# Seven block products instead of eight in the branch projections of a one-core decoder trunk

## The chip, the core and the metric

The kernel runs on one core of one Trainium2 chip. TensorE (PE) multiplies, VectorE (DVE) and ScalarE (ACT) prepare operands and take results out of PSUM, SyncE (SP) issues most DMAs and ACT the rest; GpSimd (POOL) is not used. Each engine works through its own list in order and waits on semaphores. The metric is the device time of one execution, in microseconds (us).

## The reference

512 tokens, 2048 channels, all in float32. Cut to what matters here:

```
h = rmsnorm(x); proj = h @ w_in                  # 2048 -> 18 blocks x 8 heads x 128, and 3 x 2048 gates
gates = sigmoid(proj[gate part] + gate_b)        # 3 x [512, 2048]
ya = diff_attention(...)  * silu(az)             # [512, 1024] each
yb = dilated_attention(...) * silu(bz)
yc = cb * conv3(cc * cx) * silu(cz)
merged = gates[0] * (ya @ w_branch_a) + gates[1] * (yb @ w_branch_b) + gates[2] * (yc @ w_branch_c)
out = rmsnorm(x + merged @ w_out, final_g)
```

## The kernel before

A float32 product is done as three matmuls on parts: high parts by high parts, high by low, low by high (`three`, L419 to L421). So every weight unit (128 x 1024 words, 512 KB) goes through the same line: SP loads it into one of three `raw` slots, ACT makes its high part `w_hi` (L698, L702), DVE the low part `w_lo` = raw - w_hi (L1007, L1011), PE uses both. All three tiles are rings of three, so unit r can be split only after PE is done with unit r-3, and its load can start only after the low part of unit r-3 is made.

Four stages follow each other:

- **Heads.** 8 heads, each of 18 steps (a projection block of two units, 24 matmuls each) with the attention work put between the steps. Head 0 and head 7 are written out, heads 1 to 6 are a loop. `turn` has PE transpose into two alternating PSUM tiles `tr_ps`; before turn number idx it waits until the turns up to idx-2 have been read out (`t_free`). In each head DVE forms the four weight sums for the output projection (`sum_out_units`, L1044 to L1047, at step 7): ACT loads 2 MB of `wo` into `ssum` at step 2 and stores the sums to `s_dram` at step 8.
- **Gates.** 2048 x 6144, done with 7 block products instead of 8 (a Winograd form of Strassen's scheme): 6 quads of 28 units, 12 matmuls each. The sums of the activation blocks (f1, f2, f4, f3, of 128 x 2048) are formed by DVE around the change of stage (`combine_h`, L1345, L1346) and split like weights (`comb_high`, `comb_low` L1039). The four sums of weight blocks of each quad are formed by DVE beside them (`add_units`). `take_g` (L1323) evicts a product into up to four tiles of `gin`; ACT applies tanh and stores the gates to `g_dram`.
- **Branches.** `y @ w_branch` for three branches, in 12 groups (branch, column group of 512) of 4 units, with 24 matmuls a unit: 8 k-tiles x 4 token tiles x 3. Four banks belong to a group, the other four to the next. The branch activations come from `y_dram` (`load_y`, L337, 2 MB in rows of 2 KB) and are split once per branch. `take_group` reads the four banks: (gate+1) times the bank (L1366), and for branches 1 and 2 an addition to `merged` (L1373).
- **Output.** `merged @ w_out`, transposed by PE and copied by ACT (`copy_merged`, L904), again 7 block products: 2 quads of 28 units. `take_o` (L1404) evicts; the blocks of `merged` and their sums are split at the start of this stage. A final norm follows.

The order of the work is written out by hand in each engine's program; no planner is used.

Of the kernel before, what the change touches and what calls it, by code (L numbers as in the profile page):

```python
# [58 lines left out]
GROUPS, NU = 12, 4  # L59
R_G = W1  # L60
R_B = R_G + QUADS_G * STEPS
R_O = R_B + GROUPS * NU
X_B = 8 * QUADS_G
X_O = X_B + GROUPS * NU
W11, W12, W21, W22 = range(4)
ON_X, ON_Z, ON_Y = range(3)
# [7 lines left out]
S_ORDER = [2, 3, 0, 1]  # L74
# [11 lines left out]
def spot(s):  # L86
    return S_ORDER.index(s)

# [14 lines left out]
def program(nc, wst, wg, wb, wo, x_t, x_tok, cols_d, rows_d, lam_d, const_d, out_d):  # L103
# [4 lines left out]
    s_dram = nc.dram_tensor("s_dram", (HEADS, 4, P, HU), f32, kind="Internal").ap()  # L108

    with ExitStack() as ctx:  # L110
# [74 lines left out]
        with ExitStack() as c2:  # L185
            s2 = sb_in(c2)
            s2("below2", [P, KT * T])
# [14 lines left out]
        def part(tile, n):  # L202
# [12 lines left out]
        y_parts = [[tile[:, 4096 * n:4096 * (n + 1)].rearrange("p (k q) -> p k q", k=8) for n in at]  # L215
                   for tile, at in ((tb, (0, 1)), (kb_r, (1, 2)))] + [[act_hi[:, 0:8, :], act_hi[:, 8:16, :]]]
        y_raw = kb[:, 0:4096].rearrange("p (k q) -> p k q", k=8)
        merged = act_lo_f[:, :, :].rearrange("p (s k) q -> p s (k q)", s=4)

        m_t = tb_f[:, 0:8192].rearrange("p (k q) -> p k q", k=KT)  # L220
        flat_hi = act_hi[:, :, :].rearrange("p k q -> p (k q)")
        flat_gin = gin[:, :, :].rearrange("p k q -> p (k q)")
        o11 = [part(tb, 4), part(tb, 5)]
        o_t1, o_t2, o_t4 = [[part(kb_r, n), part(kb_r, n + 1)] for n in (0, 2, 4)]
        o_t3 = [part(gin_r, n) for n in (0, 1)]
        o21, o22 = [[part(flat_hi, n), part(flat_hi, n + 1)] for n in (0, 2)]
        operands_o = [o11, o_t1, o_t2, o21, o_t3, o22, o_t4]
        g1f, g4f, g3f = part(kb, 3), part(kb, 5), part(flat_gin, 1)
        m11, m12 = [m_t[:, 0:8, h * H:(h + 1) * H] for h in range(2)]
        m21, m22 = [m_t[:, 8:16, h * H:(h + 1) * H] for h in range(2)]  # L230
        res = merged

# [5 lines left out]
        sets = [sc_ps + tr_ps, [o_ps] + pb]  # L238
# [8 lines left out]
        yraw_in, gin_in = sem("yraw_in"), [sem(f"gin_in{i}") for i in range(2)]  # L247
# [20 lines left out]
        yhi_done, ylo_done = sem("yhi_done"), sem("ylo_done")  # L268
# [20 lines left out]
        def _(sp):  # L289
# [49 lines left out]
            def load_gates(g):  # L339
                b, cg = divmod(g, 4)  # L340
                sp.dma_start(gin[:, 4 * (g % 2):4 * (g % 2) + 4, :],
                             g_dram[b, :, :, C * cg:C * (cg + 1)].rearrange("s p q -> p s q")).then_inc(gin_in[g % 2], 16)
# [28 lines left out]
            sp.wait_ge(ylo_done, 4)  # L371
            load_y(1)
            for g in range(GROUPS):
                for u in range(NU):
                    ring_free(X_B + NU * g + u)
                    load_ring(X_B + NU * g + u, wb[g, u, :, :])
                    if g < 2 and u == 3:
                        for n in range(4 * g, 4 * g + 4):
                            sp.wait_ge(g_stored[n], 16 * QUADS_G)
                        load_gates(g)  # L380
                    if g >= 2 and u == 2:
                        if g < 6:
                            sp.wait_ge(m_got, 4 * (g - 1))
                        else:
                            sp.wait_ge(m_added, 4 * (g - 5))
                        load_gates(g)
                    if g == 2 and u == 0:
                        sp.wait_ge(ylo_done, 8)
                        load_y(2)
                    if g == 3 and u == 0:  # L390
                        sp.dma_start(rows[:, :], rows_d[0:1, 3 * D:4 * D].to_broadcast([P, D])).then_inc(grow_in, 16)
            for q in range(QUADS_O):
                for n in range(STEPS):
                    p, u = divmod(n, NU)
                    x = X_O + STEPS * q + n
                    ring_free(x)
                    load_ring(x, wo[NU * q + u, (W11, None, None, W12, None, None, W22)[p], :, :] if p in (0, 3, 6) else
                              s_dram[NU * q + u, (None, W22, W11, None, W21, W12, None)[p], :, :])
# [15 lines left out]
        def _(pe):  # L414
# [173 lines left out]
            def product(r, operand, banks, p, free=None, between=None):  # L588

                hi, lo = operand  # L590
                for u in range(NU):
                    pe.wait_ge(lo_done, r + NU * p + u + 1)
                    slot = (r + NU * p + u) % RING
                    for s in range(2):
                        if free and u == 0:
                            pe.wait_ge(free[0], free[1][s])
                        for kk in range(2):
                            k, ts, cs = 2 * u + kk, slice(P * s, P * (s + 1)), slice(C * kk, C * (kk + 1))
                            end = three(banks[s][:, :], hi[:, k, ts], lo[:, k, ts], w_hi[slot][:, cs], w_lo[slot][:, cs],
                                        FRESH[p] and k == 0, k == 7, True)  # L600
                    end.then_inc(pe_used, 1)
                    if between:
                        between(u)
# [11 lines left out]
            for q in range(QUADS_G):  # L615
                for p in range(PRODUCTS):
                    if q == 0 and p in (1, 2, 4):
                        pe.wait_ge(comb_lo, {1: 1, 2: 2, 4: 4}[p])
                    product(R_G + STEPS * q, operands_g[p], pairs[(q + CHAIN[p]) % 3], p, free_g(q, p))

            def turn_merged(g, s):

                cg = g % 4
                pe.wait_ge(m_added, 4 * (g - 4) + spot(s) + 1)
                for kk in range(4):
                    end = nc.tensor.transpose(sets[g % 2][s][:, P * kk:P * (kk + 1)],
                                              merged[:, s, C * cg + P * kk:C * cg + P * (kk + 1)], ident[:, :])
                end.then_inc(m_turned, 1)

            for g in range(GROUPS):  # L630
                if g % 4 == 0:
                    pe.wait_ge(ylo_done, g + 4)
                y_hi, y_lo = y_parts[g // 4]
                for u in range(NU):
                    r = R_B + NU * g + u
                    pe.wait_ge(lo_done, r + 1)
                    slot = r % RING
                    for s in range(4):
                        if u == 0:
                            if g == 0:  # L640
                                pe.wait_ge(got, evicted(QUADS_G - 1, (5, 3)[s // 2], s % 2))
                            elif g == 1:
                                pe.wait_ge(got, evicted(QUADS_G - 1, 6, 1))
                            else:
                                pe.wait_ge(m_got, 4 * (g - 2) + spot(s) + 1)
                            if g >= 10:
                                pe.wait_ge(m_copied, 4 * (g - 10) + spot(s) + 1)
                        for kk in range(2):
                            k, ts, cs = 2 * u + kk, slice(P * s, P * (s + 1)), slice(C * kk, C * (kk + 1))
# [37 lines left out]
        def _(act):  # L687
# [219 lines left out]
            for g in range(GROUPS):  # L907
                for u in range(NU):
# [9 lines left out]
                    if g == 0:  # L918
                        high_y(1, u)
# [637 lines left out]
```

## Time and profile before

| | us |
|---|---|
| median of 3 runs (lowest, highest) | 2647.27 (2647.14, 2648.31) |
| profiled execution, own time | 2650.81 |
| its span | 2649.0 |
| PE busy | 2617.0 |
| DVE busy | 1554.4 |
| ACT busy | 866.9 |

The granted clock of PE was 0.995 of full speed over the span. A row of the timeline gives start, duration, engine, line and operation; the duration of a matmul is longer than its share of the pipe, so the pace is read from the starts. Times in all rows count from the start of the span, which begins a little after the execution's own time does.

### The profile page before, as it was taken

What the parts mean: (1) busy time and instruction counts of PE and PEld (TensorE: products, weight loads), DVE (VectorE), ACT (ScalarE), POOL (GpSimd) and SP (SyncE); (2) the same over time, 40 slices, a digit from 0 to 9 for tenths busy, and PEclk for the clock granted to TensorE, in tenths of its full rate; (3) what the DMA queues carried; (4) which work ended last, traced back from release to release, by engine and by line L of the source; (5) the groups of instructions that cost most, each with busy time, mean ns of one, the idle gap of its engine ahead of it and who ended that gap; (6) DMA issues with size and microseconds to landing.
All of it is one profiled execution on the core that took longest, in us unless ns stands there. A gap on an engine that the chain in (4) does not pass through costs nothing.

```text
span 2649.0 us, 31176 instructions
## 1 busy us (share of the span) xinstructions
PE 2617.0 (99%) x11986; PEld 2161.9 (82%) x11986; DVE 1554.4 (59%) x1910; ACT 866.9 (33%) x1089; POOL 0.2 (0%) x4
## 2 busy tenths in 40 slices
PE   8999999999999999999999999999999999999998
PEld 6888888888888888888888888878888888888786
DVE  6563654554455356365455446788877784444775
ACT  5322232322222232223232222334444443212454
POOL 0000000000000000000000000000000000000000
PEclk9999999999999999999999999999999999999999
DMA  5323333332342432333234234335455446444565
GB/s 211 119 87 100 119 123 96 119 130 85 124 131 81 135 119 87 100 120 123 96 119 130 85 124 131 135 111 191 167 185 181 161 134 246 159 144 142 186 192 195
DMA packets 102819, 359.31 MB, mean 136 GB/s; under 512 B 10017, under 2 KB 10274, under 8 KB 100770
## 3 DMA queue, kind: packets, MB, share of 16 engines
q1 hardware_dynamic: 82352, 296.49, 34.2%
q10 hardware_dynamic: 20338, 60.89, 6.3%
q8 instruction: 107, 1.75, 0.3%
q14 instruction: 22, 0.18, 0.0%
HBM read 317.50 MB, written 39.85 MB: 135 GB/s over the span
## 4 chain that ended last, share of the span: by engine, by line
PE 96%; DVE 3%; SPq 0%; DMA 0%; ACT 0%; issue 0%; DVEq 0%; ACTq 0%
PE proj L419 22%; PE proj L421 22%; PE proj L420 22%; PE sc_ps L419 3%; PE sc_ps L421 3%; PE sc_ps L420 3%; PE tr_ps L419 3%; PE tr_ps L421 3%; PE tr_ps L420 3%; PE o_ps L420 2%; PE o_ps L421 2%; PE o_ps L419 2%; PE tr_ps L460 2%; PE sc_ps L452 1%; PE o_ps L505 1%; PE sc_ps L491 1%
## 5 line engine op out<-in xcount | busy, mean ns | idle before, releaser
L419 PE MATMUL proj<-act_hi,w_hi 128*128 128x512 f32 x2304 | 910.9, 395 | 8.1 <-DVE act_lo L1055 8.1
L421 PE MATMUL proj<-act_hi,w_lo 128*128 128x512 f32 x2304 | 900.4, 391 | 0.0
L420 PE MATMUL proj<-act_lo,w_hi 128*128 128x512 f32 x2304 | 899.8, 391 | 0.0
L1007 DVE TENSOR_TENSOR w_lo<-raw,w_hi 128x1024 fp32r<-128x1024 f32 x288 | 352.7, 1225 | 400.6 <-ACT w_hi L698 400.1
L698 ACT ACTIVATE w_hi<-raw 128x1024 fp32r<-128x1024 f32 x288 | 304.6, 1058 | 842.6 <-PE proj L421 837.9
L419 PEld LDWEIGHTS proj<-act_hi,w_hi 128*128 128x128 f32 x2304 | 434.3, 189 | 96.4 <-issue 9.0
L421 PEld LDWEIGHTS proj<-act_hi,w_lo 128*128 128x128 f32 x2304 | 434.1, 188 | 92.1
L420 PEld LDWEIGHTS proj<-act_lo,w_hi 128*128 128x128 f32 x2304 | 434.7, 189 | 86.9
L1011 DVE TENSOR_TENSOR w_lo<-raw,w_hi 128x1024 fp32r<-128x1024 f32 x152 | 185.7, 1223 | 220.6 <-ACT w_hi L702 220.6
L702 ACT ACTIVATE w_hi<-raw 128x1024 fp32r<-128x1024 f32 x152 | 161.2, 1061 | 354.9 <-PE proj L421 148.2
L702 ACT ACTIVATE w_hi<-kb 128x1024 fp32r<-128x1024 f32 x120 | 127.2, 1061 | 185.2 <-PE proj L421 64.4
L1011 DVE TENSOR_TENSOR w_lo<-kb,w_hi 128x1024 fp32r<-128x1024 f32 x120 | 146.5, 1222 | 57.7 <-ACT w_hi L702 57.7
L765 ACT ACTIVATE sc<-sc,nmax 128x768 f32<-128x768 f32 (+4 forms) x96 | 65.5, 683 | 182.0 <-DVE nmax L1152 101.9
L1138 DVE TENSOR_TENSOR stage<-proj,rstd 128x512 f32<-128x512 f32 x40 | 27.6, 691 | 97.8 <-PE proj L421 97.8
L419 PE MATMUL tr_ps<-w_hi,act_hi 128*128 128x512 f32 x192 | 74.7, 389 | 0.0
L420 PE MATMUL tr_ps<-w_lo,act_hi 128*128 128x512 f32 x192 | 74.7, 389 | 0.0
L779 ACT ACTIVATE qk_hi<-stage 128x512 fp32r<-128x512 f32 x32 | 20.2, 632 | 151.7 <-DVE stage L1138 107.8
L419 PE MATMUL sc_ps<-w_hi,act_hi 128*128 128x512 f32 x160 | 63.1, 394 | 2.5 <-DVE w_lo L1011 2.5
L1136 DVE TENSOR_TENSOR stage<-proj,rstd 128x512 f32<-128x512 f32 x24 | 26.3, 1095 | 64.6 <-PE proj L421 64.6
L420 PE MATMUL sc_ps<-w_lo,act_hi 128*128 128x512 f32 x160 | 62.7, 392 | 0.0
L419 PE MATMUL sc_ps<-w_hi,tb 128*128 128x512 f32 x144 | 56.4, 392 | 1.6 <-issue 1.5
L419 PE MATMUL proj<-w_hi,act_hi 128*128 128x512 f32 x144 | 56.2, 391 | 0.9 <-DVE w_lo L1011 0.9
(294 smaller groups left out, 3343.3 us busy)
## 6 DMA issues: line engine op xcount, KB each, us to landing
raw<-wst SPq DMA_DIRECT2D x288, 512.0 KB, 3.5
raw<-wg SPq DMA_DIRECT2D x48, 512.0 KB, 4.0
raw<-wb SPq DMA_DIRECT2D x48, 512.0 KB, 3.6
kb<-wg SPq DMA_DIRECT2D x10, 2048.0 KB, 7.7
ssum<-wo ACTq DMA_DIRECT2D x8, 2048.0 KB, 9.5
s_dram<-ssum ACTq DMA_DIRECT2D x8, 2048.0 KB, 7.5
raw<-s_dram SPq DMA_DIRECT2D x32, 512.0 KB, 3.3
kb<-wg SPq DMA_DIRECT2D x24, 512.0 KB, 6.2
```

The source lines that it names most:

```text
L419: nc.tensor.matmul(out, w_h, a_h, start=first, stop=False, skip_group_check=shared)
L420: nc.tensor.matmul(out, w_h, a_l, start=False, stop=False, skip_group_check=shared)
L421: return nc.tensor.matmul(out, w_l, a_h, start=False, stop=last, skip_group_check=shared)
L452: end = nc.tensor.matmul(sc_ps[m][:, 0:n], q_part[AQ][rows, qs], k_part[AK][rows, 0:n], start=step == 0, stop=step == 2)
L460: end = nc.tensor.transpose(tr_ps[idx % 2][:, n * P:(n + 1) * P], tile, ident[:, :])
L491: end = nc.tensor.matmul(sc_ps[1][:, (g - 1) * P:g * P], blk[q][:, qs], blk[k][:, qs], start=True, stop=True)
L698: nc.scalar.activation(w_hi[slot_w][:, :], raw[slot_raw][:, :], ACT.Copy).then_inc(hi_done, 1)
L702: nc.scalar.activation(w_hi[r % RING][:, :], src, ACT.Copy).then_inc(hi_done, 1)
L765: end = nc.scalar.activation(tile[:, lo:hi], tile[:, lo:hi], ACT.Exp, scale=scale, bias=nmax[:, m:m + 1], accum_out=sums[:, m:m + 1])
L1007: tt(w_lo[slot_w][:, :], raw[slot_raw][:, :], w_hi[slot_w][:, :].bitcast(f32), ALU.subtract).then_inc(lo_done, 1)
L1011: tt(w_lo[r % RING][:, :], src, w_hi[r % RING][:, :].bitcast(f32), ALU.subtract).then_inc(lo_done, 1)
L1138: ins = tt(blk[w][:, :], pb[w % RING][:, :], rstd[:, :], ALU.mult)
```

## The change

The branch projections also get 7 block products. A branch is two quads: 4 k-tiles x 256 tokens by 4 k-tiles x 512 columns per block, so a product has 2 units of 12 matmuls and a quad 14 units. The order within a quad is P1, P2, P6, P5, P7, P3, P4. P1 and P6, P7, P4 share one chain of banks, P5 and P3 another, P2 has a third; ACT copies the first results out (`first_of`), DVE adds or subtracts the later ones (`finish`) in a tile `rows` in SBUF and then gates them.

The weight sums of the branches are formed like those of the output, in the heads: 12 + 8 sets of four sums, three sets per head (steps 7, 12 and 16; two in head 0, none in head 7). The activation sums of a branch (`sum_y`) are formed by DVE. Two of the gates' activation sums move: f4 is begun at unit 3 of the first gates quad and ended at unit 17, f3 is formed at units 8 to 11 by three operations instead of two; half of the first weight sums move from step 17 to step 16 of the last head.

```diff
-GROUPS, NU = 12, 4
+QUADS_B, STEPS_B, NU = 6, 14, 4
+ORDER_B = [P1, P2, P6, P5, P7, P3, P4]
+GATED = [0, 3, 1, 2]
+SUM_AT = {7: 0, 12: 1, 16: 2}
...
@@ SP, the loads
-            sp.wait_ge(ylo_done, 4)
-            load_y(1)
-            for g in range(GROUPS):
-                for u in range(NU):
-                    load_ring(X_B + NU * g + u, wb[g, u, :, :])
...
+            for qb in range(QUADS_B):
+                for n in range(STEPS_B):
+                    load_unit(X_B + STEPS_B * qb + n, 2 * qb + n % 2, ORDER_B[n // 2])
...
+                    if (qb, n) == (0, 9):
+                        sp.wait_ge(ylo_done, 6)
+                        load_y(1)
+                    if (qb, n) == (2, 6):
+                        sp.wait_ge(ylo_done, 7 + 6)
                         load_y(2)
...
@@ ACT, the heads
-                    if w == 2:
-                        act.dma_start(ssum[:, :, :], wo[...]).then_inc(osum_in, 16)
-                    if w == 8:
-                        act.dma_start(s_dram[...], ssum[:, :, :]).then_inc(osum_stored, 16)
+                    if w in (4, 9, 14) and not last and not (fresh and w == 14):
+                        act.dma_start(ssum[:, :, :], ws[...]).then_inc(osum_in, 16)
+                    if w - 1 in SUM_AT and not last and not (fresh and w == 17):
+                        act.dma_start(s_dram[...], ssum[:, :, :]).then_inc(osum_stored, 16)
...
@@ DVE, the heads
-                    if w == 7:
-                        sum_out_units(i)
+                    if w in SUM_AT and not last and not (fresh and w == 16):
+                        sum_units(SUM_AT[w] if fresh else 3 * i + (SUM_AT[w] - 1))
...
@@ ACT, the branches
+            def first_of(qb, p):
+                act.wait_ge(pe_used, RING + R_B + STEPS_B * qb + 2 * ORDER_B.index(p) + 2)
...
+                for s in range(2):
+                    nc.scalar.activation(parts[2 * SLOT[d] + s], bank[s][:, :], ACT.Copy, scale=float(sign)).then_inc(d_first, 1)
...
@@ DVE, the branches
+            def finish(qb, p):
+                d, first, op = {P2: (0, P1, ALU.add), P7: (3, P5, ALU.subtract), P3: (1, P6, ALU.add)}[p]
...
+                for s in range(2):
+                    tt(parts[2 * SLOT[d] + s], parts[2 * SLOT[d] + s], bank[s][:, :], op).then_inc(d_added, 1)
+                gate(qb, d)
...
+                    elif n == 0:
+                        finish(qb - 1, P3)
+                    elif n == 3:
+                        finish_last(qb - 1)
+                    if n == 6:
+                        finish(qb, P2)
+                    if n == 12:
+                        finish(qb, P7)
```

How it moves the work on DVE at two places. First, step 12 of head 0, where `w_lo` is the low part of a unit, `v_lo` reads a transposed block out of `tr_ps` and `stage` evicts the step's projection. Before:

```order
L1180 TENSOR_SCALAR pr<-sc,rsum 128x768
L1007 TENSOR_TENSOR w_lo<-raw,w_hi 128x1024
L1185 TENSOR_TENSOR v_lo<-tr_ps,v_hi 128x512
L1136 TENSOR_TENSOR stage<-proj,rstd 128x512
L1007 TENSOR_TENSOR w_lo<-raw,w_hi 128x1024
```

And now:

```order
L1253 TENSOR_SCALAR pr<-sc,rsum 128x768
L1085 TENSOR_TENSOR w_lo<-raw,w_hi 128x1024
L1122 TENSOR_TENSOR ssum<-ssum 128x1024
L1123 TENSOR_TENSOR ssum<-ssum 128x1024
L1124 TENSOR_TENSOR ssum<-ssum 128x1024
L1125 TENSOR_TENSOR ssum<-ssum 128x1024
L1258 TENSOR_TENSOR v_lo<-tr_ps,v_hi 128x512
L1209 TENSOR_TENSOR stage<-proj,rstd 128x512
L1085 TENSOR_TENSOR w_lo<-raw,w_hi 128x1024
```

The four sums now stand ahead of the read of `tr_ps` and ahead of the eviction; heads 1 to 6 have the same order. Second, the branch stage of DVE. Before, between two low parts of a group there is at most one `take_group`; here the end of a group in branch 1:

```order
L1011 TENSOR_TENSOR w_lo<-raw,w_hi 128x1024 x4
L1366 SCALAR_TENSOR_TENSOR gin<-gin,tr_ps 128x512 x2
L1366 SCALAR_TENSOR_TENSOR gin<-gin,sc_ps 128x512 x2
L1373 TENSOR_TENSOR act_lo_f<-act_lo_f,gin 128x512 x4
L1011 TENSOR_TENSOR w_lo<-raw,w_hi 128x1024 x4
```

Now, from unit 12 of quad 3 to unit 3 of quad 4 (branch 1 into branch 2; `rows` holds the partial results, `kb_r` the low part of a block of y):

```order
L1089 TENSOR_TENSOR w_lo<-raw,w_hi 128x1024
L1480 TENSOR_TENSOR rows<-rows,sc_ps 128x512 x2
L1464 SCALAR_TENSOR_TENSOR gin<-gin,rows 128x512 x2
L1471 TENSOR_TENSOR act_lo_f<-act_lo_f,gin 128x512 x2
L1089 TENSOR_TENSOR w_lo<-raw,w_hi 128x1024
L1417 TENSOR_TENSOR kb_r<-kb,kb_r 128x1024
L1089 TENSOR_TENSOR w_lo<-raw,w_hi 128x1024
L1480 TENSOR_TENSOR rows<-rows,tr_ps 128x512 x2
L1464 SCALAR_TENSOR_TENSOR gin<-gin,rows 128x512 x2
L1471 TENSOR_TENSOR act_lo_f<-act_lo_f,gin 128x512 x2
L1089 TENSOR_TENSOR w_lo<-raw,w_hi 128x1024
L1417 TENSOR_TENSOR kb_r<-kb,kb_r 128x1024
```

Six operations follow the low parts of units 12 and 0 there, each with a low part of y behind them, and a unit now has 12 matmuls and not 24.

## Rows read from the trace of the kernel before

**Rows 1.** The page: busy time and instructions; the chain that ended last, by engine.
```profile
PE 2617.0 (99%) x11986; PEld 2161.9 (82%) x11986; DVE 1554.4 (59%) x1910; ACT 866.9 (33%) x1089; POOL 0.2 (0%) x4
...
PE 96%; DVE 3%; SPq 0%; DMA 0%; ACT 0%; issue 0%; DVEq 0%; ACTq 0%
```

**Rows 2.** Windows, from the gates to the last matmul: us, busy (x), PEclk, DMA share, GB/s.
```profile
1743.31:1796.37 53.06, 47.91 (x193) 37.61 (x192) 51.95 (x44) 21.10 (x19) 0.00 (x0) 0.94 0.25 85
1796.37:2209.81 413.44, 413.44 (x1825) 342.15 (x1823) 324.80 (x310) 186.64 (x199) 0.00 (x0) 1.00 0.50 171
2209.81:2211.50 1.69, 0.16 (x1) 0.03 (x1) 1.23 (x1) 1.69 (x4) 0.00 (x0) 1.00 0.37 148
2211.50:2478.02 266.52, 266.52 (x1200) 221.46 (x1201) 119.47 (x134) 70.79 (x74) 0.00 (x0) 1.00 0.48 162
2478.02:2638.13 160.11, 156.81 (x689) 128.42 (x687) 115.16 (x114) 78.98 (x93) 0.00 (x0) 0.99 0.60 198
```

**Rows 3.** Timeline of PE, two products of a gates quad: start us, us, operation.
```profile
1807.25 0.39 PE L419 MATMUL tr_ps<-w_hi,act_hi 128*128 128x512 f32 x1
...
1818.13 0.39 PE L419 MATMUL sc_ps<-w_hi,tb 128*128 128x512 f32 x1
```

**Rows 4.** Timeline of DVE in one head: the sums, and steps 12 and 13.
```profile
971.13 1.22 DVE L1044 TENSOR_TENSOR ssum<-ssum 128x1024 f32<-128x1024 f32 x1
...
975.92 1.07 DVE L1136 TENSOR_TENSOR qk<-proj,rstd 128x512 f32<-128x512 f32 x1
...
1029.76 1.22 DVE L1007 TENSOR_TENSOR w_lo<-raw,w_hi 128x1024 fp32r<-128x1024 f32 x1 [1.78 <-ACT w_hi L698]
...
1030.90 0.68 DVE L1185 TENSOR_TENSOR v_lo<-tr_ps,v_hi 128x512 fp32r<-128x512 f32 x1
...
1034.59 1.12 DVE L1136 TENSOR_TENSOR stage<-proj,rstd 128x512 f32<-128x512 f32 x1 [3.01 <-PE proj L421]
```

**Rows 5.** Timeline of PE at the end of that step 12.
```profile
1035.52 0.82 PE L460 MATMUL tr_ps<-ident,pr 128*128 128x128 f32 x6
1036.09 0.48 PE L419 MATMUL proj<-act_hi,w_hi 128*128 128x512 f32 x1
```

**Rows 6.** Timeline of PE after the heads; in brackets the wait before.
```profile
1754.09 0.79 PE L419 MATMUL sc_ps<-w_hi,act_hi 128*128 128x512 f32 x1 [2.46 <-DVE w_lo L1011]
...
1755.54 0.63 PE L419 MATMUL sc_ps<-w_hi,act_hi 128*128 128x512 f32 x1
...
1755.97 0.63 PE L420 MATMUL sc_ps<-w_lo,act_hi 128*128 128x512 f32 x1
```

**Rows 7.** Timeline of DVE there.
```profile
1755.09 2.28 DVE L1345 SCALAR_TENSOR_TENSOR act_lo_f<-tb_f,act_hi 128x2048 f32<-128x2048 f32 x1
...
1759.62 1.22 DVE L1011 TENSOR_TENSOR w_lo<-kb,w_hi 128x1024 fp32r<-128x1024 f32 x1
```

**Rows 8.** DMA issues of SP before the branch stage: start us, us, operation.
```profile
2196.47 0.44 SPq L337 DMA_DIRECT2D kb<-y_dram  x1
2198.82 12.94 SPq L310 DMA_DIRECT2D raw<-wb  x4
```

**Rows 9.** Timeline of ACT there.
```profile
2209.08 1.06 ACT L702 ACTIVATE w_hi<-raw 128x1024 fp32r<-128x1024 f32 x1 [6.11 <-DMA raw<-wb]
```

**Rows 10.** DMA from 2195 to 2215 us: GB/s in 40 slices of 0.5 us.
```profile
GB/s 0 0 0 0 106 82 238 270 258 336 299 361 291 356 393 414 406 406 401 406 406 406 422 401 414 401 401 410 426 410 229 90 0 348 373 201 143 287 434 303
```

**Rows 11.** Timeline of DVE in the branch stage, one evicted group.
```profile
2322.90 1.28 DVE L1366 SCALAR_TENSOR_TENSOR gin<-gin,tr_ps 128x512 f32<-128x512 f32 x2
...
2325.29 2.49 DVE L1373 TENSOR_TENSOR act_lo_f<-act_lo_f,gin 128x512 f32<-128x512 f32 x4
```

**Rows 12.** Timeline of ACT in the output stage: one copy pair.
```profile
2487.42 1.06 ACT L904 ACTIVATE tb_f<-proj 128x512 f32<-128x512 f32 x2
```

**Rows 13.** Timeline of PE in the output stage: the longest wait.
```profile
2504.13 0.47 PE L419 MATMUL sc_ps<-w_hi,kb_r 128*128 128x512 f32 x1 [2.40 <-DVE act_lo_f L1404]
```

**Rows 14.** Waits of the run: us in total, times, longest us.
```profile
PE proj L419 <- DVE w_lo L1011: 0.9, 2, 0.6
```

More of the change, by code:

```diff
@@ L231, in program @@
         res = merged
+        parts = [rows[:, C * n:C * (n + 1)] for n in range(4)]
         pb = [ctx.enter_context(nc.psum_tensor(f"proj{i}", [P, T], f32)) for i in range(RING)]
@@ L585, in _, with product @@
                 blocks(i, 0)
-            def product(r, operand, banks, p, free=None, between=None):
+            def product(r, operand, banks, p, free=None, after=None, nu=NU):
                 hi, lo = operand
-                for u in range(NU):
-                    pe.wait_ge(lo_done, r + NU * p + u + 1)
-                    slot = (r + NU * p + u) % RING
+                for u in range(nu):
+                    pe.wait_ge(lo_done, r + u + 1)
+                    slot = (r + u) % RING
                     for s in range(2):
@@ L616, in _ @@
                 for p in range(PRODUCTS):
[L617 to L649, printed above, removed]
-                            end = three(sets[g % 2][s][:, :], y_hi[:, k, ts], y_lo[:, k, ts], w_hi[slot][:, cs],
-                                        w_lo[slot][:, cs], k == 0, k == 7)
-                    end.then_inc(pe_used, 1)
-                    if g >= 9 and u == 1:
-                        for s in S_ORDER:
-                            turn_merged(g - 1, s)
@@ new lines, in _, with turn_merged @@
+                    product(R_G + STEPS * q + NU * p, operands_g[p], pairs[(q + CHAIN[p]) % 3], p, free_g(q, p))
+            def turn_merged(qb, d):
+                pair = qb % 2
+                for s in range(2):
+                    n = gated(qb - 4, d, s)
+                    pe.wait_ge(m_added, gated(qb - 2, d, s))
+                    if n > 2:
+                        pe.wait_ge(m_copied, n - 2)
+                    c0 = C * (2 * pair + d // 2)
+                    for kk in range(4):
+                        end = nc.tensor.transpose(pairs[3][s][:, P * kk:P * (kk + 1)],
+                                                  merged[:, 2 * (d % 2) + s, c0 + P * kk:c0 + P * (kk + 1)], ident[:, :])
+                    end.then_inc(m_turned, 1)
@@ new lines, in turns_b, with after @@
+            def turns_b(qb, n):
+                def after(u):
+                    at = n + u
+                    if qb >= 4 and at == 8:
+                        turn_merged(qb, 0)
+                    if qb == 5 and at in (0, 2, 5):
+                        turn_merged(4, {0: 3, 2: 1, 5: 2}[at])
+                return after
+            for qb in range(QUADS_B):
+                for i, p in enumerate(ORDER_B):
+                    if qb % 2 == 0:
+                        pe.wait_ge(ylo_done, 7 * (qb // 2) + i + 1)
+                    product(R_B + STEPS_B * qb + 2 * i, operands_y[qb // 2][p], pairs[(QUADS_G + qb + CHAIN[p]) % 3], p,
+                            free_b(qb, p), turns_b(qb, 2 * i), 2)
@@ L1295, in _ @@
             head(0)
-            links = steps["n"] - before - 1
+            links = steps["n"] - before - 1 + 2
             with dve.Fori(1, HEADS - 1) as i:
```

462 lines of the change are left out of this document (277 added, 185 removed).

## The prediction

> **What bounds the kernel now.** I read the page's shares first: PE is busy 2617.0 of 2649.0 us, and the chain that ended last is PE for 96% and DVE for 3% [rows 1]. So time goes only where matmuls go or where PE waits. Then the windows by stage and, inside them, the timeline of PE for its pace and waits. The pace: two products of a gates quad, 48 matmuls, lie 10.88 us apart, 0.2267 us each [rows 3]. With it each stage can be held against its matmul count. Branch stage: 1152 matmuls x 0.2267 = 261.2, the window is 266.52 [rows 2]; the rest, 5.3 us, is 48 transposes at 0.11, so PE never waits there, DVE being busy 119 us of it. Gates, first part: 16 units should take 16 x 2.72 = 43.5 and take 53.06, a loss of 9.5. Between gates and branches 1.69 passes with one matmul in it. Output: 672 x 0.2267 = 152.3, plus 16 transposes 1.8, stands at 160.11: a loss of 6.0 [rows 2, 3]. The rest of the gates window (413.44) has 1824 matmuls x 0.2267 = 413.5 and no wait. All losses of PE after the heads are 17 us, at the changes of stage, and there DVE or a DMA is late.
>
> **The matmuls.** A branch is now 2 quads x 7 products x 2 units x 12 = 336 matmuls instead of 384; over three branches 1008 instead of 1152. 144 x 0.2267 = 32.6 us less. They are of the same shape, in a stage without waits, so all of it is on the path. Transposes stay 64. This is the one large term.
>
> **The heads.** The sums per head go from one set to three: 12 more sets in all, 4 operations each. A set takes 975.92 - 971.13 = 4.79 us on DVE [rows 4], 57 us in sum, and 48 MB more go over the ACT queue. At step 7 one set already hides. At step 16 DVE stands idle about as long as at step 12, the set delays an eviction by some 1.6, and nothing is read from `tr_ps` after it: nothing. At step 12 the set stands ahead of `v_lo`. In the trace `v_lo` starts at 1030.90, with the set at 1035.69, and ends 0.68 later at 1036.37. The eviction then starts 1.8 late (1036.3 for 1034.59); DVE had idled 3.01 before it [rows 4], and the idle time of step 13 takes up what is left. But PE's second turn after step 12 may only start when `v_lo` has read its bank. Six transposes run from 1035.52 to 1036.09, 0.095 each, so the second turn (the last two) starts at 1035.90 [rows 5]: PE waits 0.47. Seven heads have this set: +3.3. Ends: 0 (DVE's read may release earlier than its row ends; PE did not wait here before, so there is nothing to gain) and 7 x 1.8 = 12.6 if the late eviction reached PE as well. I take 3.3.
>
> **Heads to gates.** DVE is behind here: unit 3's low part comes 2.46 late, and f3's two operations (1755.09 to 1759.62, 2.27 each) stand ahead of the low part of unit 4 [rows 6, 7]. After the 2.46 wait the starts are 0.43 apart, 1.2 GHz, for eight matmuls: 1.6 us. The change takes half of f4 and two weight sums (4.6 us) out of step 17, and puts six block operations instead of five between units 3 and 13. I went through the units with 1.14 for a low part (1029.76 to 1030.90 [rows 4]), 1.13 for a weight sum, 2.2 to 2.3 for a block operation: unit 3 is late by 0.1, 4 by 1.9 (f4 before it), 5 by 1.8 (low part of the second block), then 0.4, 0.3, 0.7, 0.4, 0.4, at 14 1.8 (low part of f3) and at 15 0.9: 8.5 for 9.5 before. -1.0; ends -4 and +2 (the clock falls at these waits too).
>
> **Gates to branches.** Before the branches SP issues `load_y(1)` at 2196.47, then the first weights at 2198.82; ACT gets them at 2209.08, after 6.11 of waiting [rows 8, 9], and PE loses 1.69 - 0.2 = 1.5 [rows 2]. The load moves away from here, and the y blocks needed first were loaded one stage earlier: -1.5. It moves to unit 9 of quad 0, where its surroundings are the same: again a 2.72 us pace, again the next weight load issued 2.4 us behind 2 MB in the same queue, landing 10.1 us after its issue where 5.9 are free and 9.0 just do without PE waiting. So I put 1.5 there. `load_y(2)` was hidden before by the 5.44 us pace of a 24-matmul unit; at unit 6 of quad 2 the pace is 2.72 and it costs 1.5 as well. +3.0; ends 0 (the slices after 2203 us ran at 400 GB/s [rows 10]) and 8 (gate loads in the same queue).
>
> **Inside the branch stage.** A low part may come 3.2 us late before PE waits (5.44 for two units, less 1.06 for ACT, 1.14 for DVE); each 2.72 us step leaves DVE 1.58 for other work. A pair of 128x512 operations takes 1.2 (1.28 for two, 2.49 for four [rows 11]), so an eviction is 2.4 in branch 0 and 3.6 later, a low part of a y block 1.14. Quads 0 to 2 never pile up over 2.5. Quad 3 is worst: it makes branch 2's y blocks beside evictions of 3.6. Unit 12 starts 0.2 behind and leaves 2.2, unit 13 1.8, unit 0 of quad 4 adds 3.6 and leaves 3.8, so unit 1 is at least 0.6 late; with some 0.1 for each dependent step I take 1.2. Ends 0 and 6 (each of four such seams). At the end of quad 5 stand the sum of the first output block, two low parts (2.2 each) and evictions of 3.6: 0.6, 1.2, 3.3, 3.9 behind; the output's first product waits 1.3 for its bank, its second unit 0.6: +1.9, ends 0 and 4. Before, the same low parts lay in 5.44 us steps.
>
> **Output.** The longest wait, 2.40 [rows 13], is for the eviction of P1, behind three low parts of blocks. The change puts one more copy pair of ACT (1.06 [rows 12]) ahead of the first of them: +0.9, ends 0 and 3. The two waits of 0.9 together [rows 14] stay.
>
> **The sum.** -32.6 + 3.3 - 1.0 - 1.5 + 3.0 + 1.2 + 1.9 + 0.9 = -24.8. Profiled execution: 2650.81 - 24.8 = 2626.0. The median of the runs shown is 3.54 below that execution: 2647.27 - 24.8 = 2622.5.
>
> **Rivals.** *Waits hide better* (B): the turn in the heads is released in time, and the y loads are absorbed by the slack of the ring. 2622.5 - 3.3 - 3.0 = 2616. For it: 400 GB/s in the late slices [rows 10] against some 250 wanted. Against: the same order of loads did make PE wait once.
>
> *Short waits lower the clock* (C). PE will have about 7 waits of 0.5 in the heads and 10 of 1 to 3 later. Only waits of 2.4 us and more were followed by starts 0.43 apart; after the 1.5 us before the branches the pace stayed 0.23, and the window from there shows a clock of 1.00 [rows 2, 6]. If the five waits of 1.5 to 1.9 (the y loads, units 4, 5 and 14 of the gates) cost 1.6 each: +8, 2630.5. If every wait did: (7 + 8) x 1.6 = +24, 2646.5, no change at all (C').
>
> The Trainium skill speaks for C: "TensorE: Matmul & The Clock Gate", section "A second HAM failure mode: psum-queue depth-cycling", tells of a kernel whose PE idled for moments between matmul groups while cycling through banks and whose clock swung between its two levels. The products here now cycle three bank pairs every 24 matmuls; by that rule the sum would go to C'. The gates stage cycles the same way at a clock of 1.00 [rows 2], so the trace speaks against it as long as the waits are short.
>
> *The weight stream starves the branches* (D, slower). The stage now wants 84 x 0.524 + 24 x 0.524 (gates) + 2 x 2.1 (y) = 60.8 MB in 228.5 + 4.4 + 4.2 = 237 us, 256 GB/s; before, 162, and the output stage, the only one like it, ran at a mean of 198 [rows 2]. At 198 the stage would take 307 us: 2692. It decides against the change from 60.8 / (237 + 24.8) = 232 GB/s down. Against: slices of 400 and more over 7 us [rows 10], and the output stage lost almost nothing to its loads.
>
> The Trainium skill would add to D: "DMA: Bandwidth & Descriptors", section "Bandwidth", asks for transfers of 1 MiB and more for three quarters of the peak, and the gates now come in 24 loads of 512 KB instead of 12 of 1 MB. The sum is not changed by it: the 400 GB/s were reached with 512 KB loads in the mix.
>
> *The change does not do what it says*: the program has the 1008 matmuls; ruled out.
>
> **Chances.** Forecast 0.58 (its own range 2618 to 2628), B 0.17, C 0.13, C' 0.05, D 0.05, 0.02 for something better still. A change within 0.2%, about what a measurement of this kernel cannot tell from none, is 2642.0 to 2652.6: C' alone. Faster 0.90, same 0.05, slower 0.05. The range takes in B and C: 2614 to 2634.
>
> **What would show it.** The window from the first branch matmul to the first of the output at 237 to 240 us; a wait of about 0.5 before the transposes at step 12 of heads 0 to 6 on DVE's `v_lo`, none in head 7; a wait for a low part whose high part waited for `raw`, near units 10 of quad 0 and 7 of quad 2; one near unit 1 of quad 4 with DVE busy throughout; nothing before the first branch product. The forecast is wrong if PE waits at every seam of a quad, if the clock of the branch window is under 0.97, or if a head is longer by more than 1 us.

## The result, and the profile after

The changed kernel takes 2665.23 us (median of 4 runs, 2660.11 to 2669.44), the kernel before 2647.79 in the same comparison. The ratio is 1.0064, 95% interval 1.0053 to 1.0076: slower by 17 us, where 2622.5 had been forecast. The profiled execution of the changed kernel is its fastest, 2660.11 with a span of 2658.3; against the span before that is +9.3. Of the four runs two lie near 2661 and two near 2669; those two show a mean granted clock of 0.989 to 0.990, the profiled one 0.994, so what slows this kernel also varies from run to run.

The page of the changed kernel, the lines that answer to [rows 1]:

```profile
PE 2592.6 (98%) x11842; PEld 2134.2 (80%) x11842; DVE 1698.7 (64%) x2052; ACT 935.9 (35%) x1182; POOL 0.2 (0%) x4
...
PE 89%; DVE 5%; DMA 2%; issue 2%; ACT 1%; SPq 0%; DVEq 0%; ACTq 0%
```

PE is busy 24.4 us less, though the 144 matmuls that are gone were worth 32.6: in the branch stage it is busy 31.8 less, up to the end of the heads 7.2 more (1739.26 for 1732.03, with the same 8082 matmuls), where part of the matmuls ran at the slower clock. And the span is longer: PE now idles 66 us instead of 32, and the chain has DVE, DMA and "issue" in it. The question is where. The windows of the stages, answering to [rows 2] (first 16 units of the gates, the rest of the gates, branches, output; the passage between gates and branches is gone):

```profile
1773.88:1826.22 52.34, 46.54 (x194) 35.26 (x193) 50.88 (x43) 19.18 (x18) 0.00 (x0) 1.00 0.23 78
1826.22:2239.66 413.44, 413.44 (x1826) 342.34 (x1825) 336.53 (x320) 191.62 (x204) 0.00 (x0) 1.00 0.50 171
2239.66:2481.21 241.55, 234.74 (x1049) 192.53 (x1048) 199.73 (x221) 137.23 (x162) 0.00 (x0) 1.00 0.75 252
2481.21:2647.46 166.25, 158.46 (x696) 129.25 (x696) 116.80 (x116) 80.29 (x97) 0.00 (x0) 0.99 0.61 204
```

The branch stage is 241.55 us for 266.52, 25.0 less. The start of the gates gains 0.7, the passage to the branches 1.7, the output stage loses 6.1 (166.25 for 160.11). That is -21.3 in all, and it does not explain a slower kernel. The gates begin at 1773.88 instead of 1743.31: 30.6 us are lost in the heads, where the prediction had put 3.3.

One head of the changed kernel, from one values product to the next, cut where PE stands still:

```profile
868.23:891.68 23.45, 23.45 (x111) 19.32 (x109) 13.69 (x15) 3.19 (x3) 0.00 (x0) 1.00 0.43 152
891.68:895.09 3.41, 0.00 (x0) 0.01 (x1) 2.85 (x4) 1.58 (x2) 0.00 (x0) 1.00 0.88 268
895.09:899.66 4.57, 4.57 (x13) 3.62 (x14) 0.61 (x3) 0.00 (x0) 0.00 (x0) 0.63 0.49 179
899.66:1089.31 189.65, 189.33 (x890) 156.24 (x888) 103.91 (x144) 54.81 (x77) 0.00 (x0) 1.00 0.41 143
sum 221.08, PE 217.35 PEld 179.18 DVE 121.06 ACT 59.57 POOL 0.00; mean PE 54.34 PEld 44.79 DVE 30.26 ACT 14.89 POOL 0.00
```

The head takes 221.08 us instead of 215.25 (858.79 to 1074.04 before). PE does nothing for 3.41 us, and over the 4.6 us behind it the granted clock is 0.63 in the mean: 2.4 GHz until 896.2, then 1.2 GHz (starts 0.43 apart) until 899.6, so 13 matmuls run where 20 would fit. In the timeline of PE (start, duration, operation, in brackets the wait and what ended it):

```profile
891.29 0.39 PE L464 MATMUL proj<-act_hi,w_lo 128*128 128x512 f32 x1
895.09 0.49 PE L462 MATMUL proj<-act_hi,w_hi 128*128 128x512 f32 x1 [3.41 <-issue]
...
896.47 0.63 PE L464 MATMUL proj<-act_hi,w_lo 128*128 128x512 f32 x1
896.90 0.63 PE L462 MATMUL proj<-act_hi,w_hi 128*128 128x512 f32 x1
```

The wait ends at "issue": nothing that the profile shows as an operation was waited for. The low part that this unit needs was made by DVE long before; the second line is of ACT's queue at the end of this head:

```profile
883.02 1.21 DVE L1085 TENSOR_TENSOR w_lo<-raw,w_hi 128x1024 fp32r<-128x1024 f32 x1
```

```profile
886.41 0.38 ACTq L856 DMA_DIRECT2D s_dram<-ssum  x1
```

The place is the first matmul of a head, where PE's loop over heads 1 to 7 jumps back. The same wait stands at the start of heads 2 to 7 (3.12, 3.77, 3.41, 3.50, 3.09 and 3.86 us, 20.8 in sum) and not at the start of head 1, into which PE runs without a jump.

What PE could wait for there is its own code. The profile counts a queue q8, kind "instruction": 106 packets of 16 KB. Narrow windows of the DMA view find the packet of this place (packets, MB, share of 16 engines). In the changed kernel, 892.5 to 892.6 us:

```profile
q10 hardware_dynamic: 5, 0.02, 94.6%
q8 instruction: 1, 0.02, 58.4%
```

and in the kernel before, 879.0 to 879.1:

```profile
q8 instruction: 1, 0.02, 77.4%
```

Before, the jump is at 882.3 and the block of instructions comes 3.3 us ahead of it. After, the jump is at 891.7, so the block was due at 888.4; it comes at 892.5, 4.1 late, and PE goes on 2.6 us behind it. The same holds at the other five: the block comes at 450.0, 671.3, 1113.6, 1332.8 and 1554.3, and PE goes on 2.6 to 2.7 us behind it each time. What the DMA engines did meanwhile (GB/s in 40 slices of 0.325 us, 884 to 897 us of the changed kernel; the issues below with the KB of each and the us to landing):

```profile
GB/s 0 0 0 0 101 25 202 429 441 403 177 391 416 416 416 391 391 391 416 441 391 403 391 340 277 239 252 189 202 328 391 416 315 88 126 176 328 429 366 290
...
s_dram<-ssum ACTq DMA_DIRECT2D x1, 2048.0 KB, 8.7
raw<-wst SPq DMA_DIRECT2D x3, 512.0 KB, 4.0
```

From 886 to 892 they move 382 GB/s in the mean, 1.81 of the 2.29 MB for ACT's queue, and the 2 MB that fill them are the store s_dram<-ssum of the third set of sums, which the change put at step 17, issued at 886.41. Before, there was none at the end of a head.

### The profile page after: what moved, and what is told of

Its sections match the earlier page's. It is cut to its first block, busy times and chain, and to the rows that moved or that the text cites. A ratio compares the mean times of both kernels' runs of the same rounds, so it can differ in the third digit from the quotient of the medians.

```text
span 2658.3 us, 31420 instructions
## 1 busy us (share of the span) xinstructions
PE 2592.6 (98%) x11842; PEld 2134.2 (80%) x11842; DVE 1698.7 (64%) x2052; ACT 935.9 (35%) x1182; POOL 0.2 (0%) x4
## 4 chain that ended last, share of the span: by engine, by line
PE 89%; DVE 5%; DMA 2%; issue 2%; ACT 1%; SPq 0%; DVEq 0%; ACTq 0%
PE proj L462 20%; PE proj L464 20%; PE proj L463 20%; PE tr_ps L462 3%; PE tr_ps L464 3%; PE tr_ps L463 3%; PE sc_ps L462 3%; PE sc_ps L464 3%; PE sc_ps L463 3%; PE o_ps L463 2%; PE o_ps L464 2%; PE o_ps L462 2%; PE tr_ps L503 2%; DMA raw<-s_dram 1%; DVE w_lo L1089 1%
## 5 line engine op out<-in xcount | busy, mean ns | idle before, releaser
L1085 DVE TENSOR_TENSOR w_lo<-raw,w_hi 128x1024 fp32r<-128x1024 f32 x288 | 352.6, 1224 | 412.3 <-ACT w_hi L743 411.2
L743 ACT ACTIVATE w_hi<-raw 128x1024 fp32r<-128x1024 f32 x288 | 304.6, 1058 | 865.3 <-PE proj L464 860.5
L462 PEld LDWEIGHTS proj<-act_hi,w_hi 128*128 128x128 f32 x2304 | 435.6, 189 | 119.3 <-issue 24.4
L1089 DVE TENSOR_TENSOR w_lo<-raw,w_hi 128x1024 fp32r<-128x1024 f32 x188 | 228.9, 1222 | 112.4 <-ACT w_hi L747 112.4
L747 ACT ACTIVATE w_hi<-raw 128x1024 fp32r<-128x1024 f32 x188 | 199.3, 1061 | 259.2 <-PE tr_ps L464 68.9
L1211 DVE TENSOR_TENSOR stage<-proj,rstd 128x512 f32<-128x512 f32 x40 | 27.6, 691 | 97.8 <-PE proj L464 97.8
L462 PE MATMUL tr_ps<-w_hi,tb 128*128 128x512 f32 x200 | 78.5, 392 | 4.3 <-DVE w_lo L1089 4.2
L462 PE MATMUL sc_ps<-w_hi,tb 128*128 128x512 f32 x200 | 78.7, 393 | 3.1 <-DVE w_lo L1089 2.1
L464 PE MATMUL sc_ps<-w_hi,tb 128*128 128x512 f32 x200 | 77.9, 390 | 0.0
L464 PE MATMUL tr_ps<-w_hi,tb 128*128 128x512 f32 x200 | 77.9, 389 | 0.0
L463 PE MATMUL sc_ps<-w_lo,tb 128*128 128x512 f32 x200 | 77.9, 389 | 0.0
L463 PE MATMUL tr_ps<-w_lo,tb 128*128 128x512 f32 x200 | 77.8, 389 | 0.0
L1211 DVE TENSOR_TENSOR z<-proj,rstd 128x512 f32<-128x512 f32 x24 | 16.6, 692 | 67.3 <-PE proj L464 67.3
```

What stands on the lines that cost most here:

```text
L462: nc.tensor.matmul(out, w_h, a_h, start=first, stop=False, skip_group_check=shared)
L463: nc.tensor.matmul(out, w_h, a_l, start=False, stop=False, skip_group_check=shared)
L464: return nc.tensor.matmul(out, w_l, a_h, start=False, stop=last, skip_group_check=shared)
L743: nc.scalar.activation(w_hi[slot_w][:, :], raw[slot_raw][:, :], ACT.Copy).then_inc(hi_done, 1)
L747: nc.scalar.activation(w_hi[r % RING][:, :], src, ACT.Copy).then_inc(hi_done, 1)
L1085: tt(w_lo[slot_w][:, :], raw[slot_raw][:, :], w_hi[slot_w][:, :].bitcast(f32), ALU.subtract).then_inc(lo_done, 1)
```

## The experiments

Theory S: the store of 2 MB stands in the way of the instruction block of PE's jump. Rivals: V, the sums on DVE at step 16; W, the weight loads of the next head starved by the store, jump or not. All ratios are to the kernel before on the same chip.

**The store moved.** ACT issues the last set's store at step 1 of the next head.

```
-if w - 1 in SUM_AT and not last and not (fresh and w == 17):
-    m = SUM_AT[w - 1] if fresh else 3 * i + (SUM_AT[w - 1] - 1)
+if (w in (8, 13) and not last and not (fresh and w == 13)) or (w == 1 and not fresh):
+    m = 0 if fresh else 3 * i + {8: -1, 13: 0, 1: -2}[w]
```

> The changed kernel, with one edit: the 2 MB store of a head's last set of sums is issued at step 1 of the next head instead of step 17 of its own (for head 0 its second set). Everything else stays: the same sums at step 16 on DVE, the same number of bytes. Theory S (the store stands in the way of the 16 KB of PE instructions that are loaded when PE's loop over the heads jumps back; in the changed kernel that load is seen at 892.5 us, inside PE's wait from 891.7 to 895.1, and in the kernel before at 879.0, 3.3 us ahead of the same place): the six waits of 3.5 to 4.2 us at the start of heads 2 to 7 go, with the slower clock behind each (one head 221.08 us against 215.25). A head falls to about 215.6, the run by 6 x 5.5 = 33: 2632 of 2665, or 2627 of the profiled 2660. Rival V (the sums on DVE at step 16 make a low part or an eviction late): nothing changes, 2660 to 2665. Rival W (the weight loads of the next head are starved by the store): the waits move to step 2 of the head instead of going, 2655 to 2670.

Measured: 2632.76 us, ratio 0.9950 (0.9937 to 0.9962). The six waits are gone, and the block comes ahead of the jump again, at 878.0 for a jump at about 881.2. The head:

```profile
857.73:1073.51 215.78, 215.46 (x1011) 178.11 (x1010) 121.07 (x165) 59.58 (x82) 0.00 (x0) 1.00 0.44 150
```

215.78 us with the same operations on DVE as in the slow head. Theory S holds, V and W fall: where the store stands is worth 30.5 us between the profiled executions and 31.3 between the medians, each held against the kernel before in its own comparison (+17.4 and -13.8).

**The kernel before, with a store.** The other direction, without any sums.

```
+if w == 17 and not last:
+    act.dma_start(extra[i], ssum).then_inc(extra_stored, 16)
```

> The kernel before, with one thing added: at step 17 of heads 0 to 6 the ACT queue stores the 2 MB of ssum once more, to a place in DRAM that nobody reads. No sums are added. Theory S: a wait of about 3.6 us at the start of heads 2 to 7 (where PE's loop jumps back), none at the start of head 1 (which PE enters without a jump back), and the slower clock behind each: 6 x 5.5 = 33, 2648 + 33 = 2681. Rival V (it is the sums on DVE): 2648, no wait. Rival W (weight loads starved): waits at head 1 too, 7 x 5.5 = 38, 2686.

Measured: 2679.17 us, ratio 1.0119 (1.0105 to 1.0134), 32.6 us over the kernel before. Waits of 3.3 to 3.9 us at the start of heads 2 to 7, none at head 1, as S says and W does not. The block and the wait behind it:

```profile
q8 instruction: 1, 0.02, 58.2%
```

```profile
892.35 0.79 PE L421 MATMUL proj<-act_hi,w_hi 128*128 128x512 f32 x1 [3.27 <-DVE w_lo L1012]
```

892.35 - 889.7 = 2.6 us again, as at the other five heads. The profile names DVE's w_lo as what ended this wait; in the neighbouring heads it names "issue" for the same wait. A name in brackets is an inference, and here the jump and the packet say more.

**The same store at step 10.** The same edit with w == 10.

> The kernel before with the same additional 2 MB store per head as in the experiment that gave 2679, but at step 10 of heads 0 to 6 instead of step 17. Theory S (only a store across PE's jump back costs time, not the bytes): 2646 to 2648, no wait at the start of a head. Rival W (2 MB beside the weight stream cost PE a wait wherever they stand): 2675 to 2680.

Measured: 2646.61 us, ratio 1.0000 (0.9990 to 1.0009). 14 MB more cost nothing when no jump is near; at step 17 they cost 32.6.

**Without the third sums.** The four DVE operations at step 16 left out, load and store kept.

```
+if empty:
+    dve.sem_inc(osum_done, 1)
+    return
```

> The changed kernel without the four DVE operations of the set at step 16 in heads 1 to 6; load and store of the set stay, so a third of the weight sums are left out and the output is not the reference's. Theory S: the six waits stay, 2660 to 2665 as the changed kernel. Rival V: they go, 2630.

Measured: 2664.0 us, ratio 1.0059 (1.0044 to 1.0074), six waits of 3.2 to 3.8. V falls by itself.

**PE's loop turned.** No work moves, only the place of the jump.

```
-blocks(0, 2)
-with pe.Fori(1, HEADS) as i:
-    blocks(i, 0)
+blocks(0, 2, 12)
+with pe.Fori(0, HEADS - 1) as i:
+    blocks(i, 12)
+    blocks(i + 1, 0, 12)
+blocks(HEADS - 1, 12)
```

> The changed kernel with PE's loop over the heads written from step 12 to step 11 of the next head, so that PE jumps back at step 12 (where no 2 MB are stored or loaded by the ACT queue: the load at step 9 lands long before, the store comes at step 13) and runs straight on from one head into the next. No other engine changes, no work moves. Theory S: no wait at the start of heads 2 to 7 and none at step 12 beyond the 0.4 us that is there; about 2632. Rival W (weight loads starved by the store at the head's end) and rival V: the waits at the start of the heads stay, 2660 to 2665.

Measured: 2641.2 us, ratio 0.9976 (0.9965 to 0.9986). The waits at the start of the heads are gone though the store is still there, so it is the jump. But 2632 was expected: at the new place, step 12, waits of 0.8 to 1.7 us stand, six of them, such as

```profile
809.44 0.49 PE L462 MATMUL proj<-act_hi,w_hi 128*128 128x512 f32 x1 [1.74 <-issue]
```

Its block comes at 806.4, 3.0 us before PE goes on (2.6 to 3.1 at the six), but only 1.3 ahead of the jump where it had been 3.3 at the old place. No bulk store is about; a 512 KB weight load is, in the 2 us ahead of the block at all six (at 229, 352, 320 and 33 GB/s in the four halves of a microsecond before 806.4), while ahead of the kernel before's blocks nothing moved. Six transposes of tiles that DVE makes (`pr`) also stand right ahead of this jump. Which of the two makes the block late was not tested and stays open.

The remaining runs start from the kernel with the store moved and take the other terms.

**Sums behind v_lo** (step 12: DVE makes v_lo, then the set).

> The kernel with the store moved, and one more edit: at step 12 DVE makes v_lo first and adds the set of sums behind it. The prediction's head term said that PE's second turn waits for v_lo behind the sums; the trace shows 0.32 to 0.38 us at each of seven heads. By that theory these seven waits go: -2.5 us, 2630 (of 2632.8). Rival (the late eviction of that step reaches PE as well, or now does since it stands further back): the waits stay or turn into others of up to 1.8 each, 2633 to 2642.

Measured: 2630.2 us, ratio 0.9942 (0.9926 to 0.9958); the interval overlaps that of the kernel it starts from. In the trace the waits of the turns are gone in all heads and no other has come in the heads.

**y blocks in four parts.**

```
-load_y(1)                      # 2 MB behind unit 9 of quad 0
+load_y_part(1, n - 9)          # 512 KB behind each of units 9 to 12
```

> The kernel with the store moved, and one more edit: the two 2 MB loads of y blocks in the branch stage are issued as four loads of 512 KB each, between four weight loads. Theory Q (a weight load that is issued behind 2 MB in the same queue comes late, once in each case): the waits at 2239.1 (2.29 us) and 2308.8 (1.37 us), both for a low part whose high part waited for raw, go; with what the clock loses behind them -4 to -5 us, 2628.5. Rival D (the stream of the stage as a whole is too thin: 60.8 MB in some 240 us): the waits spread over the next units and stay in sum, 2633.

Measured: 2627.55 us, ratio 0.9931 (0.9915 to 0.9947), again with an interval that overlaps that of the kernel it starts from. Both waits are gone in the trace; of waits over half a microsecond only DVE's in quad 4 is left in the stage, 1.20 us. So the stage as a whole is not starved: its two waits came from the place of 2 MB in the queue.

**P1 evicted first.** In the output stage take_o(0, P1) at step 8, the low part of the fourth block at step 9.

> The kernel with the store moved, and one more edit: in the output stage DVE evicts P1 at step 8 and makes the low part of the fourth operand block at step 9, instead of the other way round. Theory O (the 3.8 us that P6 waits are the DVE queue ahead of P1's eviction: low parts of blocks of 2.28 and of a unit of 1.22): the wait falls by 2.28 + 1.22 = 3.5, to 0.3; with the clock behind it 2628 to 2629. Rival (the eviction then waits for the residual rows, 4 MB issued 11.0 us before it, which took 14 us to land in the median): the wait falls by less than 1.5, 2631 or more.

Measured: 2632.95 us, the median of five executions, ratio 0.9943 (0.9928 to 0.9959). One of the five, the profiled one, took 8915 us (a granted clock of 0.16 from 1277 us on); without it the median is 2632.35. No gain, which is the rival's number. Its mechanism is not shown: the waits of the output stage can't be read from a PE that ran that slowly, and in the next two kernels with this order P6's wait does fall by three microseconds and more, where the rival had it fall by less than 1.5.

**All of it, and one turn later.**

> The three edits of this call on top of the moved store, and the second turn of the output stage's first product one unit later (PE waited 2.1 us there for a copy on ACT). If the effects add up as the theories say: 2632.8 - 2.5 - 4.3 - 4.0 - 2.0 = 2620. With the rivals of each: 2628 to 2633. If the later turn only moves its wait: 2622.

Measured: 2622.57 us, ratio 0.9908 (0.9894 to 0.9922), 2.6 above the sum of the theories and near the 2622 of a turn that only moves its wait. But the turn's wait is gone and stands nowhere near it. P6 now waits 0.68 us for its bank, and its last unit waits in turn. PE, and ACT ahead of it:

```profile
2481.31 0.50 PE L468 MATMUL sc_ps<-w_hi,kb_r 128*128 128x512 f32 x1 [2.70 <-DVE w_lo L1095]
```

```profile
2478.94 1.06 ACT L753 ACTIVATE w_hi<-raw 128x1024 fp32r<-128x1024 f32 x1 [5.42 <-DMA raw<-s_dram]
```

`raw` was late: 4 MB of residual rows and 1 MB of other rows are loaded there.

**The same with those 5 MB spread** (half of the residual rows at unit 16 instead of 7, the other rows at unit 14 instead of 10).

> The kernel with all edits of the call before, and one more: at the start of the output stage the second half of the residual rows (2 of 4 MB) is loaded at unit 16 instead of unit 7, and the 1 MB load of the last rows, which the change had put at unit 10 into the queue of the weights, at unit 14. In the trace without this edit PE waits 2.70 us at 2481.3 and 1.65 at 2490.3 for low parts; at the first the high part had waited 5.42 for raw. Theory P (these 5 MB stand in the way of the weight units, and the time that the earlier eviction of P1 saves is lost there): both waits shrink to under 1 us together, 2622.6 - 4.5 = 2618. Rival (these waits are DVE's and ACT's work on the operand blocks): 2622 to 2624.

Measured: 2616.47 us, ratio 0.9886 (0.9870 to 0.9903). The waits of 0.68 and 2.70 are gone; the other, 1.65 before, has grown:

```profile
2485.72 0.50 PE L468 MATMUL o_ps<-w_hi,gin_r 128*128 128x512 f32 x1 [2.62 <-DVE w_lo L1095]
```

so theory P is right about the first and not about the second, though the time is within 2 us of its 2618. What ends the second wait in time was not followed up. This is the best version: 29.4 us under the kernel before, and some 47 under the change as it was made (which was 17.4 above it).

**P1 first with the spread, alone.**

> The kernel with the store moved and P1 evicted at step 8 (2632.95 by itself, no gain over 2632.8), and the same spread of the 5 MB. Theory P: now the eviction's place pays: P6's wait of 3.8 falls under 1 and does not come back further on, 2633 - 5 = 2628. Rival (the order of the eviction and the low part does not matter to PE, and the spread alone gives what there is): no more than 2 us, 2631.

Measured: 2630.06 us, ratio 0.9938 (0.9921 to 0.9955), between the two expectations, and its interval takes in both. P6's wait falls from 3.80 to 0.86, while the wait at P2 is 2.43 for 0.81. It is tempting to say that the wait was only shifted, but that is not shown: with P1 evicted in its old place the wait at P2 was 0.81, 1.27, 1.92 and 2.61 us in four kernels that run the same output stage (the store moved, the changed kernel, sums behind `v_lo`, y blocks in parts).

## Why the prediction was wrong

**The heads** are the step that failed. Expected +3.3, measured +30.6 in the profiled executions. The part that was worked out was right in kind and size: PE waits for v_lo at step 12, 0.3 to 0.4 us at each of seven heads (0.47 had been put),

```profile
387.93 0.44 PE L503 MATMUL tr_ps<-ident,pr 128*128 128x128 f32 x2 [0.32 <-DVE v_lo L1258]
```

and moving the sums behind v_lo took it away. What failed is the sentence on step 16: "DVE stands idle about as long as at step 12 ... nothing is read from tr_ps after it: nothing." It priced the set's DVE operations and let its DMAs pass as bytes ("48 MB more go over the ACT queue"). The store is issued at step 17, is in flight across PE's jump back, and the instruction block comes 4.1 us late. The profile before had the packet in its list (q8, "instruction") and would have shown that the block comes 3.3 us ahead of the jump; that it is needed some 2.6 ahead, so that only 0.7 us are to spare, could be read only from the runs with a wait. In the head shown the store costs 3.4 of waiting and 2.1 behind it (221.08 - 215.25 - 3.41 - 0.32 for v_lo); over the six heads, reckoned the same way, it is 20.8 and 10.7, together 31.5. Of the 10.7, 8.5 are the slower clock (3.4 us at 1.2 GHz, so 1.7 lost, in five of the heads); the rest, 0.2 to 0.5 a head, stands also where the clock never fell. Moving the store gave back 30.5 between the spans of the profiled executions. (The six heads are 33.0 us longer than six of 215.25, with five waits for v_lo in them. From that 0.5 goes, by which two heads were longer than 215.25 before, and 2.0, by which the changed kernel was ahead at the values product of head 1, 426.06 for 428.07: 30.6.) The prediction's own sign, "if a head is longer by more than 1 us", was met by 5.8.

The Trainium skill has the mechanism, in "Runtime: NRT & Kernel Launch", section "Instruction fetch mechanics": instructions stream in blocks of 16 KiB over a DMA queue, and a taken branch to a block that is not at hand "forces a DMA fetch of the target page before execution can continue". The trace agrees on the size of the packet and on PE standing still until it has come. That bulk traffic delays this fetch is what the runs here add; where the request waits meanwhile, no view shows.

**The matmuls and the branch stage** were right in kind and nearly in size: -25.0 measured for -32.6 + 3.0 + 1.2 + 1.9 = -26.5. A little of that is luck, since eight transposes, 0.9 us, went from this stage into the output stage, which was not forecast, and 0.6 of the 1.9 belongs there too: like for like it is -24.1 for -25.9. The window is 241.55 us, above the 237 to 240 given. The waits stand where they were put. The high part of unit 10 of quad 0 waits for raw behind the y load, and PE for its low part; then unit 7 of quad 2; then unit 1 of quad 4, where DVE is piled up:

```profile
2267.80 1.06 ACT L747 ACTIVATE w_hi<-raw 128x1024 fp32r<-128x1024 f32 x1 [6.91 <-DMA raw<-s_dram]
```

```profile
2270.22 0.47 PE L462 MATMUL tr_ps<-w_hi,kb_r 128*128 128x512 f32 x1 [3.20 <-DVE w_lo L1089]
```

```profile
2339.87 0.50 PE L462 MATMUL sc_ps<-w_hi,tb 128*128 128x512 f32 x1 [1.37 <-DVE w_lo L1089]
```

```profile
2401.44 0.50 PE L462 MATMUL tr_ps<-w_hi,tb 128*128 128x512 f32 x1 [1.19 <-DVE w_lo L1089]
```

The first y load was mis-sized: 3.20 us where 1.5 had been put, and 1.37 for the second (within the bounds of 0 and 8). The first is not the same in every execution: 2.29 to 4.72 us in the profiles of five other kernels that load it the same way. The seam of quads 3 and 4 is 1.19 for 1.2. The wait for the bank before the output's first product is 1.01 for 1.3. The starving of rival D did not come: D feared a supply of 198 GB/s where 256 were wanted, and the stage ran at 252.

**Heads to gates, gates to branches**: -0.7 for -1.0 and -1.7 for -1.5, right, and unit by unit too. The waits that the timeline of PE names are 1.63, 1.37, 0.44, 1.45 and 0.55. Read from the starts, as the prediction counts, the units are late by 0.3, 1.8, 1.5, 0.3, 0.2, 0.6, 0.2, 0.2, 1.6 and 0.7, where it had listed 0.1, 1.9, 1.8, 0.4, 0.3, 0.7, 0.4, 0.4, 1.8 and 0.9 (which add to 8.7; it has 8.5).

**Output** was wrong by 5: +6.1 for +0.9. PE's waits there in the changed kernel:

```profile
2481.21 0.47 PE L462 MATMUL sc_ps<-w_hi,tb 128*128 128x512 f32 x1 [1.01 <-DVE rows L1480]
...
2485.38 0.50 PE L462 MATMUL sc_ps<-w_hi,tb 128*128 128x512 f32 x1 [0.31 <-DVE w_lo L1089]
...
2490.44 0.79 PE L674 MATMUL proj<-ident,act_lo_f 128*128 128x128 f32 x5 [2.04 <-ACT act_hi_f L976]
```

```profile
2512.72 0.47 PE L462 MATMUL sc_ps<-w_hi,kb_r 128*128 128x512 f32 x1 [3.87 <-DVE act_lo_f L1533]
...
2529.49 0.50 PE L462 MATMUL o_ps<-w_hi,gin_r 128*128 128x512 f32 x1 [1.27 <-DVE w_lo L1089]
```

P6's wait is 3.87, for 2.40 + 0.9 = 3.3: that term was 0.6 short. What is not in the sum is the second turn of the first product, 2.04 us. In ACT's queue the copy that it needs stands behind a high part that waits for its weights:

```profile
2488.75 1.06 ACT L747 ACTIVATE w_hi<-raw 128x1024 fp32r<-128x1024 f32 x1 [3.39 <-DMA raw<-s_dram]
2489.72 1.07 ACT L976 ACTIVATE act_hi_f<-proj 128x512 f32<-128x512 f32 x2
```

All waits of PE in this stage come to 7.8 us (0.31, 2.04, 3.87, 1.27, 0.30) for 3.3 before (2.40, 0.57, 0.33), which is 4.5 of the 6.1; eight transposes more stand in it, 24 for 16, worth 0.9, and as many less in the branch stage; 0.7 are left. The change also moved the 1 MB load of rows out of the branch stage into the weights' queue here; the prediction priced the y and gate loads that move and missed this one. Spreading it and half of the residual rows took some 6 us off (ratio 0.9908 to 0.9886).

**Clock.** Rival C held that waits of 1.5 to 1.9 cost 1.6 each at the slower clock. The first window above has such waits (1.63, 1.45, 1.37) and a clock of 1.00, where [rows 2] showed 0.94: they cost nothing in clock. Behind five of the six waits at the heads the clock was 1.2 GHz for 3.4 us, but behind the one of 3.50 at head 5 it stayed at 2.4:

```profile
1116.26:1120.83 4.57, 4.57 (x20) 3.82 (x21) 0.52 (x3) 0.00 (x0) 0.00 (x0) 1.00 0.50 178
```

So it did behind the 3.20 at 2270, while it fell behind a wait of 1.89 in the kernel with the sums behind `v_lo`: the length of a wait alone does not tell. The same wait also differs from one execution to the next. In the profile without the third sums, 2665.5 us, the wait at head 5 is 3.50 again and the clock falls; at heads 2 and 3 it is at 1.2 GHz for 6.8 us, at heads 4 and 6 it never falls, and the first y load costs 4.72. These two are the likely cause of the spread of the runs from 2660 to 2669; no profile of a run at 2669 was taken.

## What to carry to other kernels

When a change adds a bulk transfer, look up what else needs the DMA engines in those microseconds, and count the instruction queue among it: find each engine's jump back and the 16 KB packet ahead of it, and keep 2 MB transfers clear of it. Here such a store took 8.7 us to land; issued 5.3 us ahead of the jump it cost 5.3 us a head, issued 93 us ahead or 17 us behind it cost nothing, and no distance between was tried. A wait whose releaser is "issue" (in two of six cases here the profile named DVE instead), once per loop and never at the first pass, makes a fetch the first suspect, and the cheap test is to move the transfer or the jump alone.

## What was not expected of the hardware

- An instruction block of PE was seen in the DMA queue 2.6 to 3.1 us before PE went on behind a jump, at every one of six jumps in three kernels (such as 892.5 to 895.09, 889.7 to 892.35, 806.4 to 809.44). That the packet is PE's is inferred from this, and from the wait going where the jump goes.
- With 2 MB in flight at 382 GB/s that block came 4.1 us late. The same 2 MB at step 10 or step 1 cost nothing.
- Of the six waits of 3.1 to 3.9 us, five were followed by 3.4 us at 1.2 GHz, which cost 1.7 us each, half of the wait again; the sixth, of 3.50, was followed by none.
